# Closing the blocks of a two-layer transformer kernel without the drain of GpSimd's DMA queue

## What is computed

```
def first_block(x, ...):
    for l in range(DEPTH):
        seg = {name: x @ w_in[...] ...}
        o_a = dilated_window_attention(...)
        o_b = indexer_sparse_attention(...)
        o_c, v_c = rwkv7_time_mix(...)
        o_d = mamba2_mixer(...)
        merged = sum(gates[:, :, n] * (o_n @ w_branch[l, n]))
        x = layer_norm(DEEPNORM_ALPHA * x + merged @ w_out[l], ...)
        y = hierarchical_moe(x, ...)          # top 2 of 32 experts, SwiGLU
        x = layer_norm(DEEPNORM_ALPHA * x + y, ...)
    return x

def second_block(x, c, ctx, ...):
    for l in range(DEPTH_2):
        gl_c, mq_c, mk_c, mv_c, nq_c, nk_c, nv_c = mixer_proj(h_c, ...)   # 256 context tokens
        gl, mq, mk, mv, nq, nk, nv = mixer_proj(h, ...)                   # 512 latent tokens
        y_mla = blocked_attention(...)
        y_na = neighborhood_attention(...)
        x_lat = x_lat + gt1 * gated_merge(...)
        x_lat = x_lat + gt2 * squared_relu_mlp(...)
    return x_lat
```

## Time and profile before

| | |
|---|---|
| median of 3 runs | 4047.09 us (4044.45 to 4047.91) |
| profiled execution | 4050.92 us, its span 4048.9 us |
| mean granted TensorE clock | 0.966 of full |
| TensorE busy | 3761.8 us, 93% |
| VectorE busy | 1695.6 us, 42% |
| ScalarE busy | 757.4 us, 19% |
| GpSimd busy | 168.4 us, 4% |

### The profile page before, as it was taken

One profiled execution on the slowest core, in us unless ns is written; L12 is line 12 of the kernel. 1 busy time (PEld: TensorE's weight loads), 2 busy tenths in 40 slices (PEclk: granted clock), 3 DMA queues, 4 the chain that ended last, 5 costly groups with the idle time before them and its releaser, 6 DMA issues. The chain is left out here.

```text
span 4048.9 us, 39454 instructions
## 1 busy us (share of the span) xinstructions
PE 3761.8 (93%) x15324; PEld 2203.5 (54%) x15324; DVE 1695.6 (42%) x3043; ACT 757.4 (19%) x1713; POOL 168.4 (4%) x377
## 2 busy tenths in 40 slices
PE   8988999998889999999778999999998899999999
PEld 4654788655444335555335554478544555448843
DVE  0128633545232111111265564464455556355445
ACT  1212211211132010000133442110002435111000
POOL 1001000000100000000103000000000300000000
PEclk9989999998899999999889999999999999999999
DMA  8442001315557698989623011222222101122221
GB/s 312 177 165 99 22 32 63 136 52 190 199 226 298 242 364 333 367 339 379 224 79 107 22 63 46 100 84 83 83 83 92 63 22 63 73 73 83 84 92 53
DMA packets 197389, 573.70 MB, mean 142 GB/s; under 512 B 24517, under 2 KB 34549, under 8 KB 184201
## 3 DMA queue, kind: packets, MB, share of 16 engines
q1 hardware_dynamic: 177312, 515.20, 33.9%
q10 hardware_dynamic: 12008, 29.47, 2.1%
q0 software_dynamic: 7888, 26.53, 1.8%
HBM read 540.49 MB, written 30.69 MB: 141 GB/s over the span
## 5 line engine op out<-in xcount | busy, mean ns | idle before, releaser
L346 PE MATMUL ps<-out_sums 128*128 128x256 f32 (+1 forms) x1152 | 333.6, 450 | 2.3 <-issue 2.3
L346 PEld LDWEIGHTS ps<-out_sums 128*128 128x128 f32 x1152 | 218.7, 190 | 114.2 <-issue 94.5
L346 PE MATMUL ps<-ring,mixers_xT 128*128 128x256 f32 (+2 forms) x1024 | 255.4, 404 | 13.2 <-DMA ring<-in_w_in 6.4
L346 PEld LDWEIGHTS ps<-ring,mixers_xT 128*128 128x128 f32 x1024 | 197.5, 203 | 60.9 <-issue 22.4
L346 PE MATMUL ps<-mixers_xT,ring 128*128 128x512 f32 (+1 forms) x480 | 209.2, 594 | 2.7 <-DMA ring<-in_w_in 1.7
L346 PE MATMUL ps<-ring,layers_hT 128*128 128x512 f32 x416 | 186.4, 606 | 19.6 <-PEq L276 17.2
L346 PE MATMUL ps<-ring,ctx_hT 128*128 128x512 f32 (+2 forms) x448 | 168.3, 535 | 26.8 <-PEq L127 16.6
L2282 PE MATMUL ps<-ring,mixers_xT 128*64 128x512 f32 x400 | 178.5, 603 | 5.8 <-issue 4.7
L2283 PE MATMUL ps<-ring,mixers_xT 128*64 128x512 f32 x400 | 177.5, 600 | 0.0
L346 PE MATMUL ps<-ring,out_hidden 128*128 128x512 f32 x384 | 167.4, 592 | 0.0
L346 PEld LDWEIGHTS ps<-mixers_xT,ring 128*128 128x128 f32 (+1 forms) x480 | 88.6, 187 | 117.6 <-issue 113.6
(11 more groups left out here) (852 smaller groups left out, 6169.4 us busy)
## 6 DMA issues: line engine op xcount, KB each, us to landing
ring<-in_w_ff SPq DMA_DIRECT2D x45, 2048.0 KB, 13.0
ring<-in_w_in SPq DMA_DIRECT2D x43, 2048.0 KB, 10.6
ring<-in_e_down SPq DMA_DIRECT2D x28, 2048.0 KB, 8.7
ring<-in_e_gate SPq DMA_DIRECT2D x26, 2048.0 KB, 15.6
ring<-in_e_up SPq DMA_DIRECT2D x26, 2048.0 KB, 12.5
ring<-in_w_ada SPq DMA_DIRECT2D x24, 2048.0 KB, 11.6
deep_ring_more<-in_e_up SPq DMA_DIRECT2D x7, 2048.0 KB, 9.2
deep_ring_more<-in_e_gate SPq DMA_DIRECT2D x7, 2048.0 KB, 15.5
```

The source lines that it names most:

```text
L346: last = pe.matmul(out, lhsT, rhs, start=(j == 0), stop=(j == len(pairs) - 1))
```

## The change

Each block is opened with `no_gpsimd_drain=True`.

```
@@ -273,7 +273,7 @@
-    with nc.Block() as block:
+    with nc.Block(no_gpsimd_drain=True) as block:
```

## The result

The changed kernel took 4055.79 us (median of 20 runs, 4050.65 to 4063.57) where the kernel before took 4048.91 (20 runs, 4044.45 to 4053.38): a ratio of 1.0018, with a 95% interval of 1.0011 to 1.0024. It is slower by about 7 us. The forecast was 4046.8 and its range ended at 4051.0, so the time lies outside it. The ratio is still within the 0.2% in which the forecast put it; the time is 0.6 us above the 4055.2 named there, since the three runs that the forecast started from had a median 1.8 us under that of the twenty. The profiled execution took 4056.58 us.

What follows compares the result with a forecast made beforehand. TensorE, busy 3761.8 of 4048.9 us, was taken to bound the kernel. Terms -3.55 (transposes earlier) + 2.1 (clock) + 1.1 (added instructions) = -0.35 us, from the three-run median 4047.1, gave 4046.8 us, range 4041.0 to 4051.0.

Steps and rivals of the forecast that it cites:

- Barrier opens earlier: Boundary from `wout_p` to `moe_main`: without GpSimd's drain TensorE restarts near 1042.1 us, 9.3 us earlier, the ceiling.
- Rivals 2 and 4: 2: GpSimd's semaphore waits until scatters are issued, 4044.2 us, chance 0.12; 4: barrier stays shut until they land, 4048.2 us, 0.05.
- The context matmuls: Start of `moe_main`: the 32 context matmuls keep full clock and take 13.8 us instead of 16.65.
- What is late next: First gather in `moe_main`: behind a weight load it takes 7.4 us, leaving 3.55 us gained of the 9.3.
- Rival 3: Start of `moe_main`: SyncE's early loads delay the scatters' landing, at worst 4.8 us, giving 4051.5 us; chance 0.10.
- Rival 1: First gather in `moe_main`: undisturbed, 4.6 us, and dense matmuls keep 2.4 GHz, giving 4041.8 us; chance 0.18.
- The added instructions: All 18 boundaries: one more semaphore instruction on the path, 0.06 us each, 1.1 us in all.
- The clock: First transposes and dense matmuls of `moe_main`: slow clock after 8.6 us idle costs 2.1 us, between 1.25 and 2.95.
- something outside all others: Elsewhere in the kernel: the clock's slow stretches fall differently; no size given, chance 0.05.

Runs made afterwards that it cites:

- e3: The changed kernel run again without further edits: 4055.42 us, ratio 1.0014 to the kernel before.
- e17: The changed kernel run again for a third trace: 4056.99 us in one run.
- e1: The kernel before with GpSimd's drain left out at the end of `wout_p` alone: 4052.58 us, ratio 1.0010 to the kernel before.
- e2: The kernel before with GpSimd's drain left out at the other 17 blocks, kept at `wout_p`: 4050.38 us, ratio 1.0004 to the kernel before.
- e4: The changed kernel with SyncE waiting for the first gather's landing before its expert-stage weight loads: 4054.15 us, ratio 1.0008 to the kernel before.
- e12: The changed kernel with SyncE holding its expert-stage context loads until the eight scatters have landed: 4051.50 us, ratio 1.0002 to the kernel before.
- the fill: Extra matmuls with unused results in TensorE's wait before the first transposes; ten in the changed kernel: 4047.55 us, ratio 0.9994 to the kernel before.
- e8b: The changed kernel with GpSimd waiting by semaphore in `wout_p` until the eight scatters have landed: 4049.66 us, ratio 0.9999 to the kernel before.
- e18: Second run of the changed kernel with ten extra matmuls ahead of the first transposes: 4048.25 us, ratio 0.9998 to the kernel before.
- e10: The changed kernel with SyncE waiting for the first gather before weight loads and six extra matmuls: 4044.98 us, ratio 0.9987 to the kernel before.
- e15: Rerun on another chip of the changed kernel with SyncE's wait and six extra matmuls: 4043.51 us, ratio 0.9989 to the kernel before.
- e14: The kernel before with ten fulfilled semaphore waits added on four engines in each of 17 blocks: 4052.08 us, ratio 1.0009 to the kernel before.

## Why the prediction was wrong

**Barrier opens earlier: right.** TensorE restarted 0.96 us after its last work; 0.8 was forecast, and no GpSimd drain is left. Rivals 2 and 4 are out, by the rows at 1044.6 to 1045.02 us.

**The context matmuls: right.** 13.97 us for a forecast of 13.8, with a clock of 1.0.

**What is late next: right in kind, 0.7 us off in size.** It is the gather behind the weight load, and the lead fell by 2.8 us where 3.55 was forecast (2.8 to 3.1 over changed, e3, e17 and e1, the traces in which the drain of `wout_p` was omitted and nothing added). Four terms differ: `moe_idx` went out 10.55 us after TensorE's last work instead of 9.7, its list load took 4.7 us instead of 5.4, the gather took 8.4 us instead of 7.4, and the transposes began at its landing instead of 0.4 us behind it: 0.85 - 0.7 + 1.0 - 0.4 = 0.75.

The first is the premise that the change leaves the scatters' landing where it was. It does not. The last scatter was issued 2.5 us after TensorE's last work in every trace. Where its landing is recorded, it came at 9.4 and 9.5 us with the late opening (before, e2) and at 10.1, 10.2 and 10.3 with the early one (e1, e3, e4), with `moe_idx` 0.3 us behind it, as assumed. In e3 the scatter took, for 6.9 us in the earlier trace rows,

```profile
DMA to landing us min/median/max: 7.7/7.7/7.7
```

Rival 3 has the direction, then, but not the cause: in e12, without the context loads, SyncE's wait for the same scatters ended no earlier, at 10.35 us (1051.95 less 1041.60). What else the early opening puts in their way stays open. The third term is the row that the 7.4 us came from: there the weight load went out 1.1 us ahead of the gather and not, as the text says, the same distance, 0.7; the nearer it went out, the longer the gather took. Rival 1, the undisturbed gather, did not come, but e4 shows its condition: 4.6 us without the weight load.

**The added instructions: right.** 0.060 us per boundary, read between the traces, for a forecast of 0.06.

**The clock: here the prediction failed.** The step said that the clock falls in the 8.6 us of idle time, and that the transposes and then 0.4 to 3.8 us of the dense matmuls are slow, 2.1 us in all. That part came as told: the gate was slow until 1073.5 us, and the second transposes came 18.05 us after the first instead of 15.96. But the step ended the bill there. I took "all later stages shifted by 0 to 2 us" for granted, that is, that what follows a shift runs as before. It doesn't: two further thin stretches of the context attention fell to half clock, near 1166 us (1.1 us more between the third and the fourth transposes) and from 1278 to 1292 (4.9 us), although their instructions and waits were the same. The bill for the stage was 3.2 + 4.9 = 8.1 us for a term of 2.1, whose upper end was 2.95. With a gain of 2.8 and 1.1 for the instructions this makes 6.4 us slower, for 7 measured. I had put this case at 0.05, as something outside all others, and gave it no price; it had the largest. The range could not hold it: its worst end, before I cut it, was 4052.7 us. That the restart itself cost the 2.1 us of the forecast was partly luck, as the term was the middle of 1.25 to 2.95.

The mean granted clock of one execution would not have warned of it: it is 0.966 in both profiled ones. Over all executions it does, with 0.9649 against 0.9667 to 0.9673, and beyond that it counts what lies under the slow parts. Of the slow stretch at this boundary 7.9 us fell on idle time before and 5.7 on matmuls (1043.5 to 1057.1); after, 4.7 fell on idle time and 5.5 on the transposes, the gate and the short wait between them (1063.3 to 1073.5), and the two new ones, 3.4 and 13.7 us, on an engine that worked nearly throughout.

What stays open: why the moment falls as it does in each kernel, what delays the scatters, and how much the fill gains beyond 1-5. The medians say 8 us, the traces show 3.6 in 1-5; the rest would be the executions in which the stretch near 1280 us does not come. The mean clocks agree with that, as a rough estimate: from 0.965 to 0.968 of 4050 us is 24 us less at half clock, if all else stays, of which the gate and the stretch near 1166 us are 13.6 and most of one stretch near 1280 us, 13.7, the rest. It is argued and not shown, since two traces of five do not tell how many these executions are.

## What to carry to other kernels

A barrier that opens earlier is worth only what the next late arrival leaves of it; look which transfers the earlier start issues beside that arrival. If the engine then waits at another place, ask what work stands behind the new wait, and do not end the bill at the restart. Keeping TensorE busy in a wait that can't be removed may gain more than removing another: here the removed wait gained 2.8 us of lead and the fill 3.6 us in 1-5. And where thin work follows a change of the clock closely, a tenth of a microsecond can decide on 5 us, so take two or three traces of each kernel before a slow stretch is put down to the change.

## What the runs showed of the hardware that was not expected

- GpSimd's drain waited until its own indirect DMAs had landed (13.5 us; it ended 0.4 us behind the landing, and 1.2 us in e2); a semaphore wait for the same DMAs gives the same time within 0.1% (e8b).
- A gather of token rows took 8.4 us with a 2 MB weight load issued 0.6 us ahead of it, 7.3 us at 1.3 us ahead (e18), and 4.6 us without it (e4).
- Ten extra matmuls, recorded as twenty, in a 9 us wait, with no use of their result, took a kernel from a ratio of 1.0018 to 0.9994 and 0.9998.
- Whether the clock falls in the same stretch of small matmuls can differ between two executions of one program, on two chips (e10 and e15), and costs 5 us there. Over twenty traces it fell there in all eleven in which the clock's last rise lay 12.27 us or more ahead of the fifth transposes, and in none of the nine with 12.21 or less.
- Semaphore instructions ahead of a drain ran while the engine still worked (e14) and cost about 0.03 us each by the medians, 0 to 0.09 by the interval; one behind the drain cost 0.060.
